# Sparse and forget-gate decode as one stage over one ring of tiles, and merge loads without waits

## What is computed

```
h = x + W_out( sig(gA) * W_oA(NSA(xn)) + sig(gB) * W_oB(FoX(xn)) )
y = h + W_down( gelu(causal_dwconv3(RMSNorm(h) W_up)) * (RMSNorm(h) W_gate) )
```

```python
logits = [einsum('bthd,bshd->bhts', q, k) * ATTN_SCALE + cq_t - ck  for k, _, _, ck in segs]
mask   = kpos <= qpos ;  pr = masked_softmax(logits, mask) ;  out = sum(pr_segment @ v)
```

## Time and profile before

| | us |
|---|---|
| median of 3 runs (1046.36 to 1051.4) | 1048.63 |
| the profiled execution | 1047.09 |
| its span, first to last instruction | 1044.9 |
| PE busy | 874.9 (84%) |
| DVE, ACT, POOL busy | 538.6, 355.2, 143.0 |
| DMA, mean over the span | 183 GB/s, 191.68 MB |

### The profile page before, as it was taken

One profiled execution on the slowest core, in us unless ns is written; L12 is line 12 of the kernel. 1 busy time (PEld: TensorE's weight loads), 2 busy tenths in 40 slices (PEclk: granted clock), 3 DMA queues, 4 the chain that ended last, 5 costly groups with the idle time before them and its releaser, 6 DMA issues. The chain is left out here.

```text
span 1044.9 us, 18213 instructions
## 1 busy us (share of the span) xinstructions
PE 874.9 (84%) x7327; PEld 725.0 (69%) x7327; DVE 538.6 (52%) x950; ACT 355.2 (34%) x605; POOL 143.0 (14%) x221
## 2 busy tenths in 40 slices
PE   2899368989999955556888886699997999999997
PEld 1889156878989844335666452399956898888885
DVE  5443658743433746475445240355556665665654
ACT  3222545543434322121233220244324434434431
POOL 0000300010220111412222432000000111111010
PEclk9999669999999977788999998899997999999999
DMA  5341483037422376546787999597514435535511
GB/s 194 114 166 56 148 235 129 1 113 151 160 85 82 130 293 250 204 162 257 293 323 282 395 422 412 209 251 217 156 68 165 157 122 167 195 120 177 184 40 54
DMA packets 95962, 191.68 MB, mean 183 GB/s; under 512 B 7418, under 2 KB 74778, under 8 KB 83514
## 3 DMA queue, kind: packets, MB, share of 16 engines
q1 hardware_dynamic: 80060, 87.45, 27.7%
q0 software_dynamic: 14544, 102.90, 25.3%
q10 hardware_dynamic: 1296, 0.45, 0.2%
HBM read 187.30 MB, written 7.64 MB: 187 GB/s over the span
## 5 line engine op out<-in xcount | busy, mean ns | idle before, releaser
L227 PE MATMUL banks<-tokens_turned_high,w_gates_high 128*128 128x288 f32 x320 | 96.1, 300 | 4.2 <-PEq L186 2.3
L229 PE MATMUL banks<-tokens_turned_high,w_gates_low 128*128 128x288 f32 x320 | 96.0, 300 | 0.0
L228 PE MATMUL banks<-tokens_turned_low,w_gates_high 128*128 128x288 f32 x320 | 94.6, 296 | 0.0
L958 PE MATMUL banks<-chunks_turned_high,cmp_w_high 64*128 64x256 f32 (+1 forms) x512 | 76.8, 293 | 5.4 <-DVE cmp_w_low L220 2.7
L1556 PE MATMUL banks<-consts_base,stream_rows 128*128 128x128 f32 x512 | 63.1, 285 | 15.0 <-DVE fox_keys_turned L1657 12.6
L1556 PEld LDWEIGHTS banks<-consts_base,stream_rows 128*128 128x128 f32 x512 | 59.9, 148 | 19.7 <-issue 19.3
L958 PE MATMUL banks<-chunks_turned_low,cmp_w_high 64*128 64x256 f32 (+1 forms) x512 | 73.5, 280 | 0.0
L958 PE MATMUL banks<-chunks_turned_high,cmp_w_low 64*128 64x256 f32 (+1 forms) x512 | 73.4, 280 | 0.0
L1669 ACT ACTIVATE fox_keys_turned<-banks 128x512 f32<-128x512 f32 x64 | 37.4, 597 | 96.2 <-PE banks L1633 58.6
L227 PEld LDWEIGHTS banks<-tokens_turned_high,w_gates_high 128*128 128x128 f32 x320 | 61.4, 192 | 5.2 <-issue 2.7
L228 PEld LDWEIGHTS banks<-tokens_turned_low,w_gates_high 128*128 128x128 f32 x320 | 62.2, 194 | 0.5
(11 more groups left out here) (407 smaller groups left out, 2077.1 us busy)
## 6 DMA issues: line engine op xcount, KB each, us to landing
w_up_gate<-in_w_up SPq DMA_DIRECT2D x12, 1024.0 KB
w_up_gate<-in_w_gate SPq DMA_DIRECT2D x12, 1024.0 KB
w_down<-in_w_down SPq DMA_DIRECT2D x12, 1024.0 KB, 5.1
w_in_slot<-in_w_in SPq DMA_DIRECT2D x8, 1424.0 KB, 6.1
w_gates<-in_w_in SPq DMA_DIRECT2D x16, 512.0 KB, 5.4
w_out_rows<-in_w_out SPq DMA_DIRECT2D x8, 512.0 KB, 5.2
cmp_w<-in_cmp_w_k SPq DMA_DIRECT2D x4, 512.0 KB, 20.0
cmp_w<-in_cmp_w_v SPq DMA_DIRECT2D x4, 512.0 KB
```

Source lines behind the costliest of these rows:

```text
L227: nc.tensor.matmul(out, lh, rh, start=start, stop=False, **kw)
L228: nc.tensor.matmul(out, lh, rl, start=False, stop=False, **kw)
L229: return nc.tensor.matmul(out, ll, rh, start=False, stop=stop, **kw)
L958: ins = nc.tensor.matmul(c.ps[4 + g][:, 0:w], x[rows, half * CS + 4 * q + i, :], y[k % 2][rows, i, src], start=(q + i + half + part == 0), ...
```

## The change

1. One stage `stage_decode` takes the place of the two. `decode_steps` writes out the order of 79 steps of four jobs (keys and values, NSA and FoX); `decode_ring` derives from it the order of 84 tiles of 1 MiB in a ring of seven buffers. TensorE turns step s+1 before it multiplies step s. Turned keys have four buffers in a ring, turned probabilities three.
2. An NSA tile now holds a quarter of the selected rows of four sequences (rows of 2 KB), fetched with four gathers; a window tile comes over SP.
3. FoX logits are laid out by head pair: query rows 32*j to 32*j+31 belong to pair j and four sequences. `fox_q` is zero outside of one sequence, so one tile's keys go to four column groups and accumulate over the four tiles of a group; the bias is four full-width products. A permutation (`foxbatch`) takes the place of the transpose of the probabilities.
4. The forget-gate rows are gathered at the head of the compression stage and summed there by GpSimd; the first four tiles of the ring are gathered at its end, two of them four steps earlier than the gathers of before.
5. Selection is cut into four parts between other steps; mask and distance are one tile (`dm`).
6. SP loads the first gate weights and `w_o` after the last key products and the landing of the last four tiles.
7. Merge: all eight `w_out` tiles have a buffer (four of their own, three in `hn`, one in `w_o1`) and are loaded at once, then the up and gate weights and the convolution rows; the convolution transposes move behind the first six products of the second token tile, the copies of their result behind the norms; ScalarE takes both square roots before the copies; one wait for `hcopy` is dropped.

The core of the diff, with lines left out:

```diff
+DEC_RING = 7
...
+def decode_steps():
+
+    fox = lambda half, *units: [("keys", "fox", half, i) for i in units]
+    nsa = lambda half, *units: [("keys", "nsa", half, u) for u in units]
+    fox_v = lambda half, *chunks: [("probs", "fox", half, i) for i in chunks]
+    nsa_v = lambda half, *chunks: [("probs", "nsa", half, i) for i in chunks]
+    new = lambda job, half: [("new", job, half, 0)]
+    score = lambda half: [("score", "nsa", half, 0)]
+    out = lambda job, half: [("out", job, half, 0)]
+    return (fox(0, 0, 1) + [("sums", "both", 0, 0)] + new("nsa", 0) + fox(0, 2, 3) + new("fox", 0) + fox(0, 4) + score(0) + fox(0, *range(5, 16))
+            + nsa(0, 0, 1, 2) + fox_v(0, 0, 1) + nsa(0, 3) + fox_v(0, 2) + nsa(0, 4) + fox_v(0, 3, 4)
+            + fox(1, 0, 1) + out("fox", 0) + nsa_v(0, 0, 1, 2) + fox(1, 2) + nsa_v(0, 3, 4) + fox(1, 3) + nsa_v(0, 5) + new("fox", 1)
+            + fox(1, 4) + nsa_v(0, 6) + fox(1, 5) + nsa_v(0, 7) + fox(1, 6) + new("nsa", 1) + fox(1, 7) + out("nsa", 0)
+            + fox(1, 8, 9) + score(1) + fox(1, 10) + nsa(1, 0) + fox(1, 11, 12, 13) + nsa(1, 1, 2) + fox(1, 14) + nsa(1, 3, 4) + fox(1, 15)
+            + nsa_v(1, *range(8)) + fox_v(1, *range(5)) + out("nsa", 1) + out("fox", 1))
+
+
+def decode_ring():
+
+    ring = []
+    for kind, job, half, i in decode_steps():
+        if kind == "keys":
+            ring.append((kind, job, half, i))
+        elif kind == "probs" and job == "fox" and i:
+            ring += [(kind, job, half, 4 * (i - 1) + b) for b in range(4)]
+        elif kind == "probs" and job == "nsa" and (i == 2 or i > 3):
+            ring.append((kind, job, half, max(i - 3, 0)))
+    return ring
...
+    if job == "fox":
+        table = c.d[f"cache_fox_{x}"][0].rearrange("n (r s) h e -> (n r) (s h e)", s=4)
+        b = half * 4 + i % 4
+        c.nc.gpsimd.indirect_dma_start(c.stream[r][:, :], None, table,
+                                       bass.IndirectOffsetOnAxis(ap=c.fox_row[:, i // 4, b:b + 1], axis=0)).then_inc(c.ring_in[r], 16)
...
+    table = c.d[f"cache_sel_{x}"][0].rearrange("n (r s) g h -> (n r) (s g h)", s=4)
+    for b in range(4):
+        c.nc.gpsimd.indirect_dma_start(c.stream[r][:, b * 4 * KVW:(b + 1) * 4 * KVW], None, table,
+                                       bass.IndirectOffsetOnAxis(ap=c.fox_row[:, i - 1, half * 4 + b:half * 4 + b + 1], axis=0)).then_inc(c.ring_in[r], 16)
...
+        def release(eng, n):
+
+            kind, job, half, i = ring[n]
+            if kind == "keys":
+                eng.wait_ge(turned, last_item(index[ring[n]]) + 1)
+            elif job == "fox":
+                eng.wait_ge(products, done[index[("probs", "fox", half, i // 4 + 1)]])
+            else:
+                eng.wait_ge(products, done[index[("probs", "nsa", half, i + 3 if i else 2)]])
+
...
+        @block.sync
+        def _(sp):
+            load_fox(sp)
+            load_nsa(sp)
+            load_select(sp)
+            for n, item in enumerate(ring):
+                if not window(item):
+                    continue
+                r, (kind, _, half, _) = n % R, item
+                release(sp, n - R)
+                for b in range(B4):
+                    src = d[f"state_win_{'k' if kind == 'keys' else 'v'}"][0, half * 4 + b].rearrange("(p s) g e -> p (s g e)", s=4)
+                    sp.dma_start(tiles[r][:, b, :], src).then_inc(window_in[kind, half], 16)
+            sp.wait_ge(products, done[keys[-1]])
+            for i in range(12, 16):
+                landed(sp, ("probs", "fox", 1, i))
+            load_gates(c, sp, c.gates, c.gates_in, 0)
+            load_wo(c, sp, c.wo, c.wo_in, 0)
...
+            for n in range(4, len(ring)):
+                if window(ring[n]):
+                    continue
+                if n >= R:
+                    release(pool, n - R)
+                gather_decode_rows(c, n)
...
+            def key_products(s, job, half, i):
+                t = first[s]
+                for x in (2, 3):
+                    pe.wait_ge(copied[engine[t + x]], copies[t + x])
+                k, b = divmod(i, 4)
+                if job == "fox":
+                    if b == 0:
+                        pe.wait_ge(fox_taken, fox_group(half, k))
+                    if b == 3:
+                        pe.wait_ge(bias_ready, 4 * half + k + 1)
+                        for q in range(4):
+                            nc.tensor.matmul(c.ps[4][:, q * P:(q + 1) * P], biasq[:, q, :], c.k("ident"), start=False, stop=False, skip_group_check=True)
+                    for j in range(4):
+                        ins = nc.tensor.matmul(c.ps[4][32 * j:32 * j + 32, :], fox_q(c, j, half, b), kT[kbuf[s]][:, j, :], start=(b == 0), stop=(b == 3))
+                    return ins
...
+            turn(0)
+            for s, (kind, job, half, i) in enumerate(steps):
+                if s + 1 < len(steps):
+                    turn(s + 1)
+                if kind == "keys":
+                    key_products(s, job, half, i).then_inc(products, 1)
+                if kind == "probs":
+                    value_products(s, job, half, i).then_inc(products, 1)
...
+            select_at = [[("keys", "fox", 0, i) for i in (5, 6, 7, 8)],
+                         [("keys", "fox", 1, 10), ("keys", "nsa", 1, 0), ("keys", "fox", 1, 11), ("keys", "fox", 1, 12)]]
+            take_step(0)
+            for s, step in enumerate(steps):
+                if s + 1 < len(steps):
+                    take_step(s + 1)
...
+            for b in range(DB):
+                nc.gpsimd.indirect_dma_start(c.past_logf[:, b].rearrange("p s h -> p (s h)"), None,
+                                             d["cache_fox_logf"][0].rearrange("n (e s) h -> (n e) (s h)", s=SLOTS),
+                                             bass.IndirectOffsetOnAxis(ap=c.eighth_row[:, b:b + 1], axis=0)).then_inc(c.past_logf_in, 16)
...
+            pool.wait_ge(c.past_logf_in, 16 * DB)
+            by_pair = lambda x: x.rearrange("p b (j h) -> p b j h", h=2)
+            by_row = lambda x: x.rearrange("p (j b h) -> p b j h", j=4, h=2)
+            for half in range(2):
+                lf, after = c.past_logf[:, half * 4:half * 4 + 4], c.logf_after[:, half]
+                link(nc.gpsimd.memset(after[:, SLOTS - 1], 0.0))
+                for s in range(SLOTS - 2, -1, -1):
+                    link(nc.gpsimd.tensor_tensor(by_row(after[:, s]), by_row(after[:, s + 1]), by_pair(lf[:, :, s + 1, :]), ALU.add))
+                link(nc.gpsimd.tensor_tensor(by_row(c.logf_total[:, half]), by_row(after[:, 0]), by_pair(lf[:, :, 0, :]), ALU.add))
+            for n in range(4):
+                pool.wait_ge(turned, NSTEP - 4 if n < 2 else NSTEP)
+                gather_decode_rows(c, n)
...
             for k in range(KD):
-                if k >= R:
-                    sp.wait_ge(wt_done, (k - R) // 2 + 1)
-                sp.dma_start(wt[k % R][:, :], d["w_out"][0, k * P:(k + 1) * P, :]).then_inc(wt_in[k % R], 16)
-                if k == R - 1:
-                    sp.wait_ge(w_low, 2 * KD - 2)
-                    sp.dma_start(taps_rows[0:3 * FT, :], d["conv_w"][0].rearrange("w (f p) -> (w f) p", p=P)).then_inc(conv_in, 16)
-                    sp.dma_start(taps_rows[3 * FT:4 * FT, :], d["conv_b"][0].rearrange("(f p) -> f p", p=P)).then_inc(conv_in, 16)
-                    sp.dma_start(st_rows, d["state_ffn_conv"][0].rearrange("b w f -> (b w) f")).then_inc(conv_in, 16)
-                    ffn.load_up_gate(sp, 0, 0)
-                    ffn.load_down(sp, 0, 0)
+                if k == KD - 1:
+                    sp.wait_ge(w_low, 2 * KD)
+                sp.dma_start(wt[k], d["w_out"][0, k * P:(k + 1) * P, :]).then_inc(wt_in[k], 16)
+            ffn.load_up_gate(sp, 0, 0)
+            sp.dma_start(taps_rows[0:3 * FT, :], d["conv_w"][0].rearrange("w (f p) -> (w f) p", p=P)).then_inc(conv_in, 16)
+            sp.dma_start(taps_rows[3 * FT:4 * FT, :], d["conv_b"][0].rearrange("(f p) -> f p", p=P)).then_inc(conv_in, 16)
+            ffn.load_down(sp, 0, 0)
+            sp.wait_ge(wt_done, 2)
+            sp.dma_start(st_rows, d["state_ffn_conv"][0].rearrange("b w f -> (b w) f")).then_inc(conv_in, 16)
 
...
-                if k == 5:
-                    pe.wait_ge(conv_in, 48)
-                    nc.tensor.transpose(c.ps[5][:, 0:4 * FT], taps_rows, c.k("ident")[0:4 * FT, 0:4 * FT])
-                    for f in range(FT):
-                        ins = nc.tensor.transpose(c.ps[6][:, f * 2 * DB:(f + 1) * 2 * DB], st_rows[:, f * P:(f + 1) * P], c.k("ident")[0:2 * DB, 0:2 * DB])
-                    ins.then_inc(conv_turned, 1)
...
+                    if (n, k) == (0, 5):
+                        pe.wait_ge(conv_in, 48)
+                        nc.tensor.transpose(c.ps[5][:, 0:4 * FT], taps_rows, c.k("ident")[0:4 * FT, 0:4 * FT])
+                        for f in range(FT):
```

(16 more changed lines are left out.)

929 lines of the change are left out of this document (416 added, 513 removed).

## The result

| | median, us | before beside it | ratio |
|---|---|---|---|
| the changed kernel | 1063.7 (1059.6 to 1065.6, 4 runs) | 1047.5 | 1.0147, 95% interval 1.0116 to 1.0178 |

The forecast was 987 us, faster; the kernel became slower by 16 us. The profiled execution took 1059.59 us at a span of 1057.4. First the page: the span and two rows of its 40 slices. The weak region of the old profile is still there, from the 15th to the 26th slice: TensorE falls to 4 and 5 tenths in it, and DMA is seldom at 9.

The account below looks back on a forecast made before the run. TensorE, DMA and waits took turns as decode's bound; side by side, 224.5 us from 377.1 to last landing puts merge at 614.1, not 670.8 (-56.7). Merge -5 gives 985.4, plus 1.5 for the median: 987 us, range 962 to 1015.

Parts of the forecast that it names:

- TensorE 2.91 us a key tile, VectorE hides behind it: FoX key tiles in the decode stage: turning ahead removes 1.56 us of waiting per four; VectorE's 1.6 us a tile hides.
- Rival B: Hand-over in the decode stage: copies still arrive late, costing 16 us plus 8 us at four softmaxes; 1011 us, chance 16%.
- I follow the ring tile by tile: Seven-buffer decode ring: tile n is gathered when tile n-7 is released; a FoX value chunk releases four tiles at once.
- part 2: Decode stretch of five NSA key tiles and four chunks of FoX values: 44.5 us, written out tile by tile.
- GpSimd has 155 us of gathers inside the stage, in lumps: Decode gather issue: 1.25 us each whatever the size; 64 small and 60 large gathers take 155 us of GpSimd.
- part 3: Decode stretch of eight FoX key tiles with NSA values between: GpSimd sets the pace, 6.25 us a pair, 35 us.
- D: Decode window tiles on SP's starved queue stop the ring: 4 x 25 = 100 us at 43 us each; 1087 us, chance 2%.
- C: Small NSA gathers in decode: 3.0 us between latency and transfer not overlapped, 152 us over 16 tiles; about 1135 us, chance 3%.
- A: Transfers alone bound decode: issue and chunks hidden, NSA rows at 426 GB/s; 973 us, or 967 with 6.4 us hidden; 12%.
- E: Decode stays in turns, value chunks waiting for a softmax that waits for the last key tile; 1035 to 1045 us, 3%.
- Before and behind the stage: Around decode: early forget-gate gathers add 6.4 us; last landing to merge takes 12.5, 4 from late gates; merge saves 5.
- parts 4 and 5: End of decode: eight FoX key tiles, five NSA, then all second-half values, paced by GpSimd, then transfers: 86 us.

Follow-up runs that it names:

- the paced run: Changed kernel with one gather for an NSA tile, GpSimd kept busy 3.7 us behind each by ten chained fills: 1023.0 us, 0.9928 of the kernel before.

## Why the prediction was wrong

The sum of the causes, in us of the stage from its start to the merge stage:

| | length | of the 77 us |
|---|---|---|
| changed kernel, hold-up present | 314.1 | |
| changed kernel, hold-up absent (377.3 to 658.7) | 281.4 | 32.7 hold-up |
| eight buffers, values first, early gates, hold-up absent (378.3 to 631.5) | 253.2 | 28.2 ring and order (some 2 of it behind the last landing) |
| forecast | 237.0 | 16.2 rest |

Each length is that of one trace. The medians of the changed kernel in the two conditions are 37.5 us apart and the traced spans 27.5, so the first share is known to some 5 us.

1. **"TensorE 2.91 us a key tile, VectorE hides behind it": right.** 2.89 us. Rival B (copies late, 24 us) did not come about: TensorE waits for copies of keys for 5 us in all.
2. **"I follow the ring tile by tile": the term that was mis-sized without any hold-up.** I charged a chunk of values 5.5 us of latency and 3 of products. Two things were left out. TensorE turns step s+1 before it multiplies step s; I used that where it helps, and not where a chunk's products, and with them the release of four buffers, stand behind the transposes of a key tile that is gathered after the chunk's own last tile. And a gather behind a release shares the queue with three or four others, so that a median of 7.4 us passes to its landing in part 2, and 9.7 for the key tile of the second wait, not the least latency of the earlier trace rows. A chunk took 15 to 20 us where 8.5 were charged. From the first NSA product to the first transposes of the second half (forecast 44.5 us):

| kernel | us |
|---|---|
| changed (440.1 to 502.3) | 62.2 |
| one gather, no hold-up (431.9 to 492.3) | 60.3 |
| values first (440.1 to 497.7) | 57.6 |
| both (436.1 to 490.6) | 54.5 |
| both, eight buffers, second time (441.3 to 489.0) | 47.6 |

The order of turning is 5 us of it, the eighth buffer 7, and the gathers 2 to 3; 3 us are left to the forecast. The forecast was for seven buffers, so these 7 us are what a ring of seven costs beside one of eight, and my working tile by tile did not have them.
3. **"GpSimd has 155 us of gathers inside the stage, in lumps": right as a pace, blind as to the engines beside it.** The spacing of 1.25 us held, and the pace is worth 8 us. What I did not see is that other engines can be held up during such a run. It was in the profile of before: ScalarE's "<-remote" and TensorE's 3.04 us "<-issue" at 432 stood in the stretch from which the earlier trace rows has its last gather. I read the rows of GpSimd there and not those beside them. The change has 64 small gathers, in runs of up to 15, where before there was one run of 12 and others of four to six. Of the 25 us by which part 3 exceeded its 35, 13 are this (60.2 with the hold-up, 47 without), 6 the ring (41) and 6 open.
4. **Rivals.** D (slower by the window tiles) gave the right sign for a wrong reason: TensorE never waits for one. C was the nearest in its object, small gathers, and wrong in mechanism and size (its sum, 987 + 152, is 1139 and not 1135): the gathers overlap, and without the hold-up one gather of 1 MiB at the pace of four is no faster than the four of 256 KB (0.9928 and 0.9927). The sign that I had named for C and D, a wait for an NSA tile of over 5 us, did appear (10.1 us), but from the release of the ring, so it was no sign of either. A and E did not come about: DMA was busy for 0.77 of the stage, and TensorE's longest wait for turned probabilities was 3.1 us. The Trainium skill, "DMA: Bandwidth & Descriptors", section Bandwidth, asks for at least 1 MiB a transfer; one gather of 1 MiB is indeed better here, by 42 and by 8 us. The fixed 2.0 us of that page (section "Anatomy of one DMA") are not what is paid: of a tile's four gathers each costs GpSimd 1.25 us of issue, 5.0 in all, and the rest overlaps.
5. **Before and behind the stage: right within 3 us.** The first product of the compression stage came at 223.08 (forecast 223 to 225), the stage began at 374.4 (377.1), and the merge stage gave 5.2 us in the trace and 5.1 alone. Of the 12.5 us behind the last landing 11.0 came, and the late load of the gates was 1.7 us of them, not 4.
6. **The rest of 16 us** is 7.5 us in part 2, 6 in part 3 and 6 in parts 4 and 5, less 3 behind them. In parts 4 and 5 the DMA share is 0.96 at 368 GB/s, so the transfer is likely the bound there, and it runs below the 426 GB/s at which I priced a FoX tile; whether this is all of it was not tried, and the rest of part 2 and part 3 stays open.

Without the hold-up the result was 0.9927 of before: the right sign, and still 39 us from the forecast (which was 0.941 of its kernel before). The step that failed, then, is the ring as I followed it: the cycle of a chunk of values, and GpSimd's lumps taken as harmless to the engines beside them.

## What to carry to other kernels

For each release of a buffer write down everything that stands ahead of it in its engine's order, and when the data of *that* was asked for: a look-ahead that helps where products are the bound delays releases where transfers are. A trace holds its own warnings: idle time with no releaser, on several engines at once, is a cause to be priced before a change multiplies what runs beside it. And when the kernel before changes its time by more than the effect, compare across groups of runs only where it took the same time.

## What the runs showed of the hardware

While GpSimd issues gathers back to back, every 1.25 us, the other engines may react late: TensorE issues one product in 0.7 to 2 us, and ScalarE starts a copy 7.5 (kernel before) or 9.4 us (changed kernel) after the transposes that it waits for, at the least. It goes with long rows of gathers, and not with the rows of memory in each: 64 gathers of 128 rows and 64 of 32 rows both have it (16.6 and 23.2 us of TensorE's idle time), and with one gather a tile, never more than six in a row inside the stage, it all but disappears (0.3 to 2.2 us). Whether it is their number or the time for which GpSimd issues without a pause is not separated, since the paced run met the other condition. And it goes with a condition that the kernel does not set: without it 36 gathers in a row hold up nobody, and the kernel before took 1047 to 1049 us in groups 1, 2 and 5 and 1031 to 1033 in groups 3 and 4, and one chip had it in group 1 and not in group 3. What sets this condition, and by which path an engine is held up, these runs do not show. The Trainium skill, "SBUF — State Buffer", section "SBUF: two separate sides", has the ports of engines and DMA as disjoint, so that neither slows the other, and has VectorE and GpSimd alone share a port. The page speaks of ports only. No run here shows whether a port has a part in it, and by a port or not, TensorE does lose time beside gathers: 16.6 us of its own idle time in the trace of the changed kernel, against 0.4 in the other condition.
